# Down projections of a four-part feed-forward as seven block products, with weight sums made by adding DMAs

## The chip, the cores and the metric

The kernel runs on one core of one Trainium2 chip. The metric is the device time of one execution in microseconds (us). Engines: TensorE (PE; PEld is its weight load), VectorE (DVE), ScalarE (ACT), GpSimd (POOL), SyncE (SP, which only issues DMAs here).

## What is computed

One inference step of a two-layer encoder over T = 640 tokens (512 of a new stream, 8 x 16 of running streams), D = 1024, all in float32. The reference holds four feed-forwards (two in each layer), differential attention in the first layer, forgetting attention in the second, a shared K/V projection between them, and a final norm. What matters here:

```
def swiglu(x, w_gate, w_up, w_down):
    return (jax.nn.silu(x @ w_gate) * (x @ w_up)) @ w_down
...
x = x + 0.5 * swiglu(rms_norm(x, g), w_gate, w_up, w_down)    # w_gate, w_up: 1024 x 2816, w_down: 2816 x 1024
```

## The kernel before

**Numbers and halves.** Every matmul works on rounded parts: a weight and an operand are each split into a high part (a ScalarE copy to fp32r) and a low part (a VectorE subtraction), and hi x hi, hi x lo and lo x hi are added in PSUM. A product of 128 x 128 weights with half of the tokens (320) is thus three matmuls, of 320 columns each. The norm's root (rB) is multiplied in after the matmul, as it is one factor per token.

**A feed-forward** (f = 0 to 3) goes through 11 pairs of 128-wide hidden blocks in four groups of 2, 3, 3 and 3 pairs (GROUPS). For each group come first the gate and up columns, then the down projection of that group, which is added to the residual xT.

**Gate and up: sets of seven products.** A set is 256 columns of gate (even s) or up (odd s). Its weights are seen as a 2 x 2 of blocks W11, W12, W21, W22 (rows 0 to 511 and 512 to 1023 by 128 columns each), the tokens as two halves, and seven products in place of eight give the result. Their weights are the ROLES: W11, W12, W22 and the sums S1 to S4; their operands are called "1" to "7" (sums of parts of x, made once for each feed-forward). VectorE makes the four sums in `role_sum` (L2018), ScalarE the high parts in `role_high` (L1446), VectorE the low parts in `role_low` (L2004). Each role has one slot (ROLE_SLOT), which is free again when its product of the set before is through. `products` (L78) writes the order out: product S4 and product W22 of set s stand between those of set s + 1. TensorE's product is L780. Between products ScalarE copies a partial sum from one PSUM bank to another (`copy_rows`, L1526), which the next product then adds to: three copies for each set, and S2, S3 and W22 wait for them. VectorE reads the results in `first_rows`, `sums_out` and `last_rows`; ScalarE makes the silu (L1542) and the hidden high part (L1549), VectorE the hidden low part (L2196).

**Down: plain.** For each of eight output tiles of 128 rows, `ffn_down` (L886) multiplies all hidden blocks of the group with their weights, three matmuls for each block and token half. VectorE then scales with rB (L2246), adds half of it to xT (L2248) and, in the last group, goes on to the next operand (`low`, L1979, and the sum of squares, L1990), as ScalarE does in `finish` (L1420, L1425).

**Order.** Each engine's program is written out by hand; the class `Plan` counts what each semaphore has reached. All queues are in order: a waiting instruction holds back what is behind it. SP loads the weights into two raw buffers in turn (`load_ffn`, `set_load`); a raw buffer is free when its last split is done. GpSimd does nothing in the feed-forwards; it splits the weight tiles of qkv, kv and qb (L657, L659) and serves attention.

## Time and profile before

| | |
|---|---|
| median of 3 runs | 2509.86 us (2508.21 to 2512.95) |
| the profiled execution, its own time | 2508.48 us |
| its span | 2506.2 us |
| TensorE busy | 2457.8 us, 98% of the span, 18869 matmuls |
| VectorE, ScalarE, GpSimd busy | 1696.2, 1136.8 and 193.6 us |
| granted TensorE clock | 0.997 |
| HBM read, written | 246.56 MB, 13.51 MB |

The busy times overlap between engines. The chain of waits goes back from the last instruction to whatever released each step; an engine's idle time costs only where it stands on that chain.

### The profile page before, as it was taken

The page shows a single profiled execution, that of the slowest core. Times are in us where ns is not written, and L with a number is a line of the kernel's source. Part 1 is how long each engine was busy: PE and PEld are TensorE (multiplying, and loading weights), DVE is VectorE, ACT ScalarE, POOL GpSimd, SP SyncE. Part 2 cuts the span into 40 slices and gives each one's busy share as a digit, 9 for nine tenths or more (in the row PEclk, how much of TensorE's full clock was granted, in tenths as well). Part 3 has the DMA queues.
Part 4 walks back from the last instruction along what each step waited for, and adds up shares of the span by engine and source line. Part 5 has one row for each costly group of instructions (what it writes and reads, how often), then busy time and mean ns, then how long its engine had stood idle before and what let it go on. Part 6 is the DMA issues. An engine that isn't in the chain of part 4 may idle for free.

```text
span 2506.2 us, 46841 instructions
## 1 busy us (share of the span) xinstructions
PE 2457.8 (98%) x18869; PEld 2332.4 (93%) x18869; DVE 1696.2 (68%) x2966; ACT 1136.8 (45%) x2263; POOL 193.6 (8%) x140
## 2 busy tenths in 40 slices
PE   8999999999998999999999999999999999999998
PEld 8999999888678999999988999999996699999998
DVE  7777677322787876767624886858628787868585
ACT  6443444201785644434422643435418754535254
POOL 0000000344000000000054000000131000000000
PEclk9999999999999999999999999999999999999999
DMA  4323232232863132323224232322257531322222
GB/s 129 92 72 95 70 100 60 76 118 93 293 235 96 60 101 64 98 65 97 66 73 139 95 110 60 104 80 77 72 179 254 215 109 47 112 79 74 87 72 80
DMA packets 261489, 262.99 MB, mean 105 GB/s; under 512 B 13537, under 2 KB 222106, under 8 KB 261282
## 3 DMA queue, kind: packets, MB, share of 16 engines
q1 hardware_dynamic: 255536, 244.98, 31.4%
q10 hardware_dynamic: 5746, 15.12, 1.7%
q8 instruction: 146, 2.39, 0.4%
q14 instruction: 61, 0.50, 0.1%
HBM read 246.56 MB, written 13.51 MB: 104 GB/s over the span
## 4 chain that ended last, share of the span: by engine, by line
PE 90%; DVE 5%; ACT 3%; issue 2%; DMA 0%; POOL 0%; ACTq 0%; DVEq 0%; POOLq 0%
PE PS L780 40%; PE PS L886 24%; PE PS L967 10%; PE PS L730 7%; PE PS L718 2%; PE PS L1168 1%; PE PS L713 1%; PE PS L1025 1%; PE PS L1126 1%; PE PS L1087 1%; ACT R L1681 0%; ACT tt L1689 0%; DVE x_area L2063 0%; DVE tt L2375 0%; DVE R L2018 0%
## 5 line engine op out<-in xcount | busy, mean ns | idle before, releaser
L780 PE MATMUL PS<-x_area,w_area 128*128 128x320 f32 x3096 | 482.1, 309 | 0.0
L780 PEld LDWEIGHTS PS<-x_area,w_area 128*128 128x128 f32 x3096 | 461.0, 188 | 0.2 <-DVE w_area L2004 0.2
L886 PE MATMUL PS<-r_area,w_area 128*128 128x320 f32 x2568 | 393.3, 309 | 0.0
L886 PEld LDWEIGHTS PS<-r_area,w_area 128*128 128x128 f32 x2568 | 380.6, 188 | 0.8 <-DVE r_area L2196 0.8
L1446 ACT ACTIVATE w_area<-R 128x512 fp32r<-128x512 f32 x341 | 212.9, 629 | 200.6 <-PE PS L780 133.4
L1995 DVE TENSOR_TENSOR w_area<-R,w_area 128x768 fp32r<-128x768 f32 (+2 forms) x145 | 134.8, 929 | 218.9 <-ACT w_area L1431 217.4
L2004 DVE TENSOR_TENSOR w_area<-R,w_area 128x512 fp32r<-128x512 f32 x341 | 233.9, 686 | 47.6 <-ACT w_area L1446 41.5
L1431 ACT ACTIVATE w_area<-R 128x768 fp32r<-128x768 f32 (+2 forms) x145 | 119.1, 822 | 310.1 <-PE PS L886 283.1
L967 PE MATMUL PS<-w_area,xn_hi 128*128 128x512 f32 x800 | 252.1, 396 | 2.7 <-POOL w_area L659 2.7
L886 PE MATMUL PS<-v_area,w_area 128*128 128x320 f32 x1620 | 253.5, 309 | 0.0
L886 PEld LDWEIGHTS PS<-v_area,w_area 128*128 128x128 f32 x1620 | 241.5, 188 | 0.3 <-DVE v_area L2196 0.3
L2018 DVE TENSOR_TENSOR R<-R 128x512 f32<-128x512 f32 x336 | 230.3, 685 | 4.0 <-DMA R<-in_w_ffn_gate_dram 1.6
L780 PE MATMUL PS<-k_area,r_area 128*128 128x320 f32 x1296 | 206.8, 309 | 0.0
L2004 DVE TENSOR_TENSOR r_area<-R,r_area 128x512 fp32r<-128x512 f32 x259 | 177.2, 689 | 40.4 <-ACT r_area L1446 37.7
L1446 ACT ACTIVATE r_area<-R 128x512 fp32r<-128x512 f32 x259 | 161.7, 625 | 86.9 <-DVE R L2018 78.3
L780 PEld LDWEIGHTS PS<-k_area,r_area 128*128 128x128 f32 x1296 | 194.3, 188 | 0.3
L967 PEld LDWEIGHTS PS<-w_area,xn_hi 128*128 128x128 f32 x800 | 147.7, 189 | 31.5 <-POOL w_area L659 2.8
L657 POOL CAST w_area<-R 128x1024 fp32r<-128x1024 f32 x48 | 53.4, 1113 | 1560.6 <-PE PS L886 950.6
L1526 ACT ACTIVATE PS<-PS 128x320 f32<-128x320 f32 x258 | 106.8, 418 | 135.4 <-PE PS L780 134.9
L780 PE MATMUL PS<-x_area,r_area 128*128 128x320 f32 x1032 | 165.4, 309 | 0.5 <-issue 0.5
L967 PE MATMUL PS<-w_area,xn_lo 128*128 128x512 f32 x400 | 156.7, 392 | 0.0
L780 PEld LDWEIGHTS PS<-x_area,r_area 128*128 128x128 f32 x1032 | 154.8, 188 | 0.7 <-issue 0.7
(302 smaller groups left out, 3569.9 us busy)
## 6 DMA issues: line engine op xcount, KB each, us to landing
R<-in_w_ffn_up_dram SPq DMA_DIRECT2D x88, 512.0 KB, 3.9
R<-in_w_ffn_gate_dram SPq DMA_DIRECT2D x84, 512.0 KB, 3.9
R<-in_w_ffn_down_dram SPq DMA_DIRECT2D x96, 384.0 KB, 3.2
vreg<-in_cache_a_v_dram SPq DMA_DIRECT2D x8, 2048.0 KB, 9.0
vreg<-in_cache_b_v_dram SPq DMA_DIRECT2D x8, 2048.0 KB, 8.8
R<-in_cache_a_k_dram SPq DMA_DIRECT2D x14, 1024.0 KB, 6.8
R<-in_cache_b_k_dram SPq DMA_DIRECT2D x14, 1024.0 KB, 8.8
R<-in_w_qkv_a_dram SPq DMA_DIRECT2D x24, 512.0 KB, 3.8
```

The lines of the kernel that those rows point to most:

```text
L657: pool.tensor_copy(w_hi[slot][:, 0:words], raw[slot][:, 0:words]).then_inc(w_hi_made, 1)
L718: return pe.transpose(dst, src[rows], cst[rows, IDENT + 64 * r:IDENT + 64 * r + 64])
L730: last = pe.matmul(out[:, h, :], a[slot][:, w], x[:, k, h * HT:(h + 1) * HT], start=(k == 0 and a is w_hi and x is x_hi), stop=(k == kb - ...
L780: last = pe.matmul(PS[:, bank, 0:HT], a[:, k, :], b[:, k, :], start=(start and k == 0 and a is hi and b is x_hi), stop=(k == 3 and a is lo ...
L886: last = pe.matmul(out[:, h, :], a[slot][:, w], x[:, h * HT:(h + 1) * HT], start=(k == 0 and a is w_hi and x is hi), stop=(k == n - 1 and ...
L967: last = pe.matmul(PS[:, t, :], x[:, k, cols], a[s][:, w], start=(k == 0 and x is xn_hi and a is w_hi), stop=(k == KB - 1 and x is xn_lo))
L1431: act.activation(w_hi[p][:, 0:words], raw[p][:, 0:words], ACT.Copy).then_inc(w_cast, 1)
L1446: act.activation(role_parts(f, g, s, role)[0], role_source(f, g, s, role), ACT.Copy).then_inc(sem("early_cast") if key in EARLY_COUNT else ...
L1526: act.activation(PS[:, to, 0:HT], PS[:, of, 0:HT], ACT.Copy).then_inc(sem("copied"), 1)
L1995: dve.tensor_tensor(w_lo[p][:, 0:words], raw[p][:, 0:words], w_hi[p][:, 0:words].bitcast(F32), ALU.subtract).then_inc(w_split, 1)
L2004: dve.tensor_tensor(lo, role_source(f, g, s, role), hi.bitcast(F32), ALU.subtract).then_inc(sem("early_split") if key in EARLY_COUNT else ...
L2018: dve.tensor_tensor(*at, ALU.add).then_inc(w_summed, 1)
```

## The change

1. *Down projections* of all groups but the last one of the last feed-forward (PLAIN) become sets of the same kind. A down set is 256 output rows; there are four (DOWN_SETS) for each group, with a contraction over the group's pairs, so 2 or 3 blocks deep (`depth`) in place of 4. The operands "1" to "7" are now made from the hidden rows for each pair (`hidden_sum`, `hidden_parts_low`, `hidden_cast`): four sums, five casts (parts 1, 5, 7 with 6, 2 with 3, 4) and five low parts. The 0.5 and rB are multiplied into the gate (`gate_scaled`), and VectorE adds the results straight to xT.
2. *One chain of sets* runs through a whole feed-forward (`chain`). The down set that opens a group's down part does not interleave with the set before it: TensorE first finishes the last up set (S4, W22), then takes W11, S1, S2, W12, S3 of the down set (`opening_down`).
3. *Weight sums.* S1 = W21 + W22, S3 = W11 + W21 and, for gate and up, S4 = S2 + W12 are made by DMAs that GpSimd issues and that add a block from DRAM to one that lies in SBUF (`add_sums`). VectorE keeps S2 = S1 + W11, S4 of the down sets, and S1 of the first set in three feed-forwards. S2 and S4 share one buffer (`sums`), so the S2 sum of a set waits for the S4 split of the one before.
4. *Ends.* In the last group of feed-forwards 0 to 2, the next operand's tiles are made two at a time at the end of a down set (`finish_tile`, `finish_one`), and the following projection starts with `set_done` waits. The first two tiles of kv and qb are split by ScalarE and VectorE.
5. *Room.* kT (2560 KB) is stored to DRAM after kv and loaded back in qb; mask and rope constants are loaded by ScalarE's queue when qkv begins.

```diff
+DOWN_SETS = KB // 2
+PLAIN = ((3, len(GROUPS) - 1),)
+HIDDEN_PARTS = ("1", "5", "7", "2", "4")
...
-        self.tiles("kv", ROW_TILES)
+        self.tiles("kv", ROW_TILES, range(2))
...
+            def add_sums(f):
+
+                def first_sum(at):
...
+                    pool.wait_ge(w_loaded[p], PLAN.landed[key])
...
+                    pool.dma_start(role_source(*key, "S1"), weight_block(*key, 1, 1), accum_op=ALU.add).then_inc(sem("first_added"), 16)
+
+                def third_sum(at):
+                    key = (f, *at)
+                    pool.wait_ge(w_summed, PLAN.sum[(*key, "S2")])
+                    if (*key, "W11") not in EARLY_COUNT:
+                        pool.wait_ge(w_split, SPLIT[(*key, "W11")])
...
+                    pool.dma_start(role_source(*key, "S3"), weight_block(*key, 0, 1), accum_op=ALU.add).then_inc(sem("third_added"), 16)
...
+                order = chain(f)
+                first_sum(order[0])
+                for at, then in zip(order, order[1:] + [None]):
+                    third_sum(at)
+                    if then is not None:
+                        first_sum(then)
+                    fourth_sum(at)
...
+            def opening_down(f, g, s):
+
+                i = PLAN.set[f, g, s]
+                q, v, first_rows = s % 2, 2 + s % 2, 4 + s % 2
+                pe.wait_ge(sem("sum_read"), i - 1)
+                product(f, g, s, "W11", "1", q, True)
+                product(f, g, s, "S1", "5", v, True)
+                pe.wait_ge(sem("copied"), 3 * i + 1)
+                product(f, g, s, "S2", "6", q, False)
+                product(f, g, s, "W12", "2", first_rows, False)
+                pe.wait_ge(sem("copied"), 3 * i + 2)
+                product(f, g, s, "S3", "7", q, False)
...
             sp.wait_ge(w_used, BASE["qb"])
-            sp.wait_ge(stored, STORED["bv"])
+            sp.wait_ge(stored, STORED["kt"])
...
+            sp.dma_start(kT[:, :, :].rearrange("p h t -> p (h t)"), k_scr).then_inc(sem("v_back"), 16)
```

**ScalarE after an up part of three pairs (feed-forward 0, group 1).** From the cast of W11 of the second down set (D1) on; L1630 is the cast of a role, L1727 of a hidden part, L1715 a PSUM copy; `third_added` is the adding DMA of S3. Of the change:

```order
L1630 ACTIVATE r_area<-R2 128x384 [waits w_used,w_loaded1]
L1630 ACTIVATE w_area<-R1 128x384 [waits w_used,w_summed]
L1727 ACTIVATE v_area<-vN 128x320 [waits hidden_ready]
L1630 ACTIVATE r_area<-R2 128x384 [waits w_used,first_added]
L1715 ACTIVATE PS<-PS 128x320 [waits sum_read,w_used]
L1630 ACTIVATE r_area<-R1 128x384 [waits w_used,w_summed]
L1630 ACTIVATE w_area<-R2 128x384 [waits w_used,w2_loaded0]
L1630 ACTIVATE w_area<-R2 128x384 [waits w_used,w2_loaded1]
L1630 ACTIVATE w_area<-R2 128x384 [waits w_used,third_added]
L1715 ACTIVATE PS<-PS 128x320 [waits last_rows_read,w_used]
L1715 ACTIVATE PS<-PS 128x320 [waits first_rows_read,w_used]
```

The last two rows, D0's third and D1's first PSUM copy, stand behind the cast that waits for the adding DMA. Before, ScalarE had at this place the casts of plain down tiles (L1431) and two hidden high parts (L1549):

```order
L1526 ACTIVATE PS<-PS 128x320 [waits sum_read,w_used]
L1534 ACTIVATE R1<-PS 128x320 [waits sum_read,w_used]
L1446 ACTIVATE w_area<-R2 128x512 [waits w_used,w2_loaded1]
L1542 ACTIVATE tt<-tt 128x640 [waits gate_ready]
L1526 ACTIVATE PS<-PS 128x320 [waits last_rows_read,w_used]
L1431 ACTIVATE w_area<-R2 128x768 [waits w_used,w_loaded0]
L1549 ACTIVATE v_area<-tt 128x640 [waits hidden_ready] x2
```

**VectorE at the same place.** L2491 and L2499 are hidden sums, L2520 hidden low parts, L2268 role low parts, L2286 weight sums, L2479 the last up rows. Of the change:

```order
L2491 TENSOR_TENSOR vN<-tt 128x320 [waits dve_step,first_rows_read]
L2499 SCALAR_TENSOR_TENSOR vN<-tt 128x320
L2499 SCALAR_TENSOR_TENSOR vN<-tt,vN 128x320 [waits dve_step]
L2520 SCALAR_TENSOR_TENSOR v_area<-vN,v_area 128x320 [waits hidden_hi]
L2479 TENSOR_TENSOR tt<-tt,PS 128x320 [waits last_rows_read,w_used]
L2499 SCALAR_TENSOR_TENSOR vN<-tt,vN 128x320 [waits hidden_ready,last_rows_read]
L2520 SCALAR_TENSOR_TENSOR v_area<-vN,v_area 128x640 [waits hidden_ready,hidden_hi]
L2520 SCALAR_TENSOR_TENSOR r_area<-tt,r_area 128x640 [waits hidden_hi,dve_step,last_rows_read]
L2268 TENSOR_TENSOR r_area<-R2,r_area 128x384 [waits w_cast]
L2268 TENSOR_TENSOR w_area<-R1,w_area 128x384 [waits w_cast]
L2520 SCALAR_TENSOR_TENSOR v_area<-vN,v_area 128x320 [waits hidden_hi]
L2286 TENSOR_TENSOR R1<-R2 128x384 [waits first_added,w_split]
```

The last row is the S2 sum of D1, which releases the adding DMA for S3; it stands behind the sums and low parts of the last pair. Before, the same place had:

```order
L2169 TENSOR_TENSOR tt<-PS,R1 128x320 [waits fifth_copied,copied,w_used]
L2170 TENSOR_TENSOR tt<-PS,R1 128x320
L2178 TENSOR_TENSOR tt<-tt 128x640 [waits silu_done,sum_read,last_sum_read]
L2188 TENSOR_TENSOR tt<-tt,PS 128x320 [waits last_rows_read,w_used]
L2196 SCALAR_TENSOR_TENSOR v_area<-tt,v_area 128x640 [waits hidden_hi] x2
```

Two hidden low parts (x2) were all that followed the up rows there.

## Rows read from the trace of the kernel before

**Rows 1.** The page, section 1: busy time, share of the span, instructions

```profile
PE 2457.8 (98%) x18869; PEld 2332.4 (93%) x18869; DVE 1696.2 (68%) x2966; ACT 1136.8 (45%) x2263; POOL 193.6 (8%) x140
```

**Rows 2.** The chain of waits: start us, us, what; feed-forward 0, then qkv

```profile
102.89 73.92 PE PS L780 x504
176.81 42.24 PE PS L886 x288
...
451.37 13.64 PE PS L967 x60
```

**Rows 3.** Windows view, an up stretch and a down stretch of three pairs

```profile
core 0: us, PE busy (x) PEld busy (x) DVE busy (x) ACT busy (x) POOL busy (x), PEclk, DMA share, GB/s
102.89:176.81 73.92, 73.92 (x507) 73.92 (x506) 59.94 (x99) 39.21 (x73) 0.00 (x0) 1.00 0.24 69
176.81:219.05 42.24, 42.24 (x291) 42.24 (x290) 24.88 (x33) 10.13 (x14) 0.00 (x0) 1.00 0.35 106
```

**Rows 4.** Groups of VectorE, then ScalarE, by shape: busy us, mean ns | idle before

```profile
L2018 DVE TENSOR_TENSOR R<-R 128x512 f32<-128x512 f32 x336 | 230.3, 685 | 4.0 <-DMA R<-in_w_ffn_gate_dram 1.6
...
L2175 DVE TENSOR_TENSOR tt<-tt,rB 128x640 f32<-128x640 f32 x43 | 35.5, 826 | 4.8 <-DVE tt L2170 0.5
...
L1995 DVE TENSOR_TENSOR w_area<-R,w_area 128x1024 fp32r<-128x1024 f32 x17 | 20.8, 1223 | 4.4 <-ACT w_area L1431 4.4
...
L1446 ACT ACTIVATE w_area<-R 128x512 fp32r<-128x512 f32 x341 | 212.9, 629 | 200.6 <-PE PS L780 133.4 <-DVE R L2018 67.1
...
L1526 ACT ACTIVATE PS<-PS 128x320 f32<-128x320 f32 x258 | 106.8, 418 | 135.4 <-PE PS L780 134.9 <-issue 0.5
...
L1425 ACT ACTIVATE tt<-xT 128x640 f32<-128x640 f32 x47 | 34.0, 723 | 0.0
...
L1420 ACT ACTIVATE xn_hi<-xT,gT 128x640 fp32r<-128x640 f32 x24 | 20.0, 831 | 62.2 <-DVE xT L2248 62.2
```

**Rows 5.** Timeline of VectorE: start us, us, engine, line, operation

```profile
229.62 0.48 DVE L2156 TENSOR_TENSOR tt<-PS,rB 128x320 f32<-128x320 f32 x1
230.02 0.68 DVE L2018 TENSOR_TENSOR R<-R 128x512 f32<-128x512 f32 x1
230.62 1.47 DVE L2004 TENSOR_TENSOR w_area<-R,w_area 128x512 fp32r<-128x512 f32 x2
...
234.20 0.82 DVE L2175 TENSOR_TENSOR tt<-tt,rB 128x640 f32<-128x640 f32 x1
234.94 0.68 DVE L2004 TENSOR_TENSOR w_area<-R,w_area 128x512 fp32r<-128x512 f32 x1
```

**Rows 6.** DMA view: issues, KB each, median us to landing

```profile
R<-in_w_ffn_gate_dram SPq DMA_DIRECT2D x84, 512.0 KB, 3.9
R<-in_w_ffn_down_dram SPq DMA_DIRECT2D x96, 384.0 KB, 3.2
...
R<-in_w_ffn_down_dram SPq DMA_DIRECT2D x32, 256.0 KB, 2.8
...
vN<-out_dram SPq DMA_DIRECT2D x1, 2048.0 KB, 9.0
...
R<-in_x_sample_dram SPq DMA_DIRECT2D x4, 128.0 KB, 7.1
...
R<-in_w_f_b_dram SPq DMA_DIRECT2D x1, 64.0 KB, 2.2
```

**Rows 7.** Timelines of TensorE and VectorE at the start

```profile
58.37 1.87 PE L780 MATMUL PS<-v_area,r_area 128*128 128x320 f32 x11 [1.69 <-DVE r_area L2004]
...
57.63 0.68 DVE L2004 TENSOR_TENSOR r_area<-R,r_area 128x512 fp32r<-128x512 f32 x1
```

**Rows 8.** Timelines of GpSimd in qkv, SP's queue and TensorE before attention B

```profile
466.29 2.33 POOL L659 TENSOR_TENSOR w_area<-R,w_area 128x1024 fp32r<-128x1024 f32 x1 [6.88 <-issue]
...
1847.00 0.38 SPq L635 DMA_DIRECT2D vN<-out_dram  x1
...
1869.69 0.49 PE L1025 MATMUL PS<-kT,R 64*128 64x128 f32 x4
```

More of the change, by code:

```diff
@@ L103, in __init__ @@
         self.ffn(2)
-        self.tiles("qb", SQ_TILES)
+        self.tiles("qb", SQ_TILES, range(2))
         self.tiles("ob", SQ_TILES, range(SQ_TILES))
@@ new lines, in ffn @@
+        order, turned, base = chain(f), self.loads % 2, self.units
+        if f == 0:
+            for s in range(2):
+                for role, slot in STANDARD[s]:
+                    self.role((0, 0, s, role), slot)
+                    self.own((0, 0, s, role))
+                    self.split[0, 0, s, role] = self.unit[0, 0, s, role] + 1
+            base = self.units
+        for (g, s), role in products(f):
+            slot = ROLE_SLOT[role]
+            self.role((f, g, s, role), slot[:2] + str(1 - int(slot[2])) if turned and len(slot) == 3 else slot)
@@ new lines, in ffn @@
+        for n, ((g, s), role) in enumerate(splits(f)):
+            self.split[f, g, s, role] = base + n + 1
+            self.own((f, g, s, role))
+        for g, s in ([(0, 0), (0, 1)] if f == 0 else []) + order:
+            key, early = (f, g, s), f in EARLY and (g, s) == (0, 0)
+            p = self.next_load(key, not early)
+            if not early:
+                self.halves[p] += 1
+                self.landed2[key] = 16 * self.halves[p]
+                for part, last in ((1, "S3" if (g, s) in order else "W21"), (2, "W22")):
+                    self.raw_free[key, part] = self.raws.get((p, part), 0)
+                    self.raws[p, part] = self.split[f, g, s, last]
@@ L169 @@
+        for g, pairs in enumerate(GROUPS):
+            for k in range(pairs):
+                self.pair[f, g, k] = len(self.pair)
+                parts = HIDDEN_PARTS if (f, g) not in PLAIN else range(2)
+                self.hidden.update({(f, g, k, x): len(self.hidden) + n + 1 for n, x in enumerate(parts)})
+            if (f, g) in PLAIN:
+                self.tiles((f, g), KB, range(KB))
 PLAN = Plan()
-UNIT, LOAD = PLAN.unit, PLAN.load
+UNIT, LOAD, SPLIT = PLAN.unit, PLAN.load, PLAN.split
@@ L826, in first_pair, with set_rest @@
                 pe.wait_ge(sem("first_gate"), 2)
[L828 to L832 removed]
+            def set_rest(f, g, s):
+                product(f, g, s, "S4", "3", 6, False)
+                pe.wait_ge(sem("copied"), 3 * PLAN.set[f, g, s] + 3)
+                product(f, g, s, "W22", "4", 7, False)
```

942 lines of the change are left out of this document (608 added, 334 removed).

## The prediction

> **What bounds the kernel now.** I read the page first: TensorE is busy 98% of the span [rows 1]. Busy matmuls could still hide pauses, so the second view is the chain of waits [rows 2]: in the feed-forward parts it is TensorE alone, 504 matmuls in 73.92 us and 288 in 42.24 us, both 0.1467 us each, without a pause between groups. The third is the windows view [rows 3]: in such a stretch VectorE is busy 59.9 of 73.9 us, ScalarE 39.2, GpSimd not at all, and the granted clock is 1.00, its 2.4 GHz level. So only fewer matmuls, or a stall of TensorE, move the time there. One pause exists at the start, 1.7 us [rows 7].
>
> **What goes.** A pair of hidden blocks (256 wide) needs 8 output tiles x 2 blocks x 3 partial products x 2 halves = 96 down matmuls now; as four sets of seven products with three partial products each it needs 84. 41 of the 44 pairs change: 41 x 12 = 492 matmuls, at 0.1467 us [rows 2] **72.2 us less** on the path. Also 255 of the 344 weight sums (0.685 us; 336 are of one form, [rows 4]) leave VectorE, and 240 operations that update x; both lie beside TensorE now and save nothing by themselves.
>
> **What comes beside TensorE.** The spacing of independent VectorE operations is 0.40 us for 320 columns, 0.60 for 512 and 0.74 for 640 [rows 5]; by these ends 0.47 for 384 and 0.34 for 256 (my interpolation). A down set of three pairs takes TensorE 63 x 0.1467 = 9.24 us and VectorE 7 low parts and 2 sums of 384, 6 additions of 320: 6.6 us. With two pairs it is 6.16 against 5.5 us. That fits, so I cost the work itself at nothing; what costs is the order in which it has to come.
>
> **The price of an adding DMA, X**, from the sum on VectorE that releases it to its landing, is in no row. Plain loads land in 2.8 us for 256 KB, 3.2 for 384 and 3.9 for 512, in rows of 1 KB; 64 KB take 2.2 [rows 6]. The changed DMAs carry 128, 192 (down) and 256 KB (up). Lowest bound: a plain load of the same bytes, 2.4 / 2.6 / 2.8 us. But they also read their destination: a load of twice the bytes gives 2.8 / 3.2 / 3.9. They move pieces of 512 bytes, half of today's: if the part above 2.1 us, about what 64 KB take, doubles once more, 3.5 / 4.3 / 5.7. The far bound is the 7.1 us in which 128 KB land in the crowded first microseconds [rows 6]. I take a point a third of the way from the second to the third triple, **3.0 / 3.6 / 4.5**, since some of that slope is waiting behind other loads. The Trainium skill, DMA: Bandwidth & Descriptors (Anatomy of one DMA), gives a GpSimd DMA about 2.0 us plus its bytes at 436 GB/s; by that, as an estimate, X is 2.3 / 2.45 / 2.6 and the time that of the cheap rival below. No run here shows it.
>
> **Where TensorE will wait.** Count from the end of product S3 of the last up set of a group (0).
> - *Opening.* The S3 weights of the first down set D0 can only be split now (0.47 + 0.5 us); then VectorE does the gate scaling 0.74, sum S4 0.47, a low part 0.40, the up rows 0.8 and a dependent 0.83 (spacing and durations of [rows 4, 5]), hidden sums 5, 7, 6 (1.4 with their dependence) and low part 5: 6.2 us. TensorE has meanwhile S4 and W22 (3.52 us), W11 of D0, and S1 but for the last pair: 5.7 us with three pairs, 4.8 with two. It waits 0.6 or 1.4 us. Low part 7 is ready at 8.0, TensorE at 7.6 or 7.2: 0.4 or 0.9. Together **1.0 us** (three pairs) or **2.3 us** (two).
> - *Second down set D1.* After low 7 VectorE does low 2, W11, S4, low 4 and then the S2 sum of D1, ready at 10.6 (10.2). Only now may the adding DMA for its S3 start. ScalarE's cast of S3 waits for it, and behind that cast in ScalarE's queue stand the two PSUM copies, of which the second releases S2 of D1: 10.6 + X + 1.35 us. TensorE is there at 8.5 + 5 products = 15.1 (12.9 with two pairs: 10.2 + X + 1.25). It waits for X - 3.15, or X - 1.45: 0.45 or 1.55 us.
> - *The loop.* From the landing of one S3 sum to the next S2 sum VectorE and ScalarE take about 3.5 us in order; with X that is 7.1 against a set of 9.24 us, nothing; with two pairs 6.45 against 6.16, 0.3 us, twice. The next up set's 256 KB sum starts from the same loop and has room for 3.2 us: X = 4.5 costs 1.3. Later up sets have 12.3 us per set against X + 5 to 6.3, nothing.
> - So a three-pair opening costs 1.0 + 0.45 = 1.45 us, eleven of them **16.0**; a two-pair one 2.3 + 1.55 + 0.6 + 1.3 = 5.75, four of them **23.0**.
> - *Last group of the first three feed-forwards.* After each S3 cast ScalarE now makes two tiles of the next operand: 2 x (0.83 + 0.72) us [rows 4], one square waiting for VectorE, so the PSUM copies come 3.0 us later and the next sum later too. Room is left for X up to 2.65 at D2 and 2.15 at D3: 0.95 + 1.45; then the first weight tile of the next projection is split late (1.06 + 1.22 us against two products of 1.32, behind that work): 1.0. 3 x 3.4 = **10.2**.
> - *Start.* VectorE's split of a weight releases TensorE there [rows 7]. It loses two sums of 0.6 and gains two scalings of 0.74 and, ahead of the next split, four hidden sums and five low parts instead of two, less one S4 sum: 0.3 + 0.4 + 2.7 - 0.6, with dependences **3.3 us** more pause.
> - *Keys through DRAM.* 2560 KB more come back behind the values in SP's queue, issued at 1847.0 us; 2048 KB of values take 9.0 us to land, so with the 512 KB of the running streams all three land at about 1847.0 + 22.5 = 1869.5, and the first scores start at 1869.7 [rows 6, 8]: **1.0**, bounds 0 and 6. The store itself has two up sets, 24.6 us, before the first wait for it: nothing.
> - Masks and rope constants loaded later, and GpSimd relieved of two tiles each in kv and qb: covered by the first projection tiles, which take TensorE 13.6 us in qkv [rows 2], nothing; without that cover up to the 6.9 us that GpSimd's first subtraction is late in qkv [rows 8].
>
> **Sum.** -72.2 + 16.0 + 23.0 + 10.2 + 3.3 + 1.0 = -18.7. The profiled execution took 2508.5 us (span 2506.2), the median of the runs is 1.4 above: 2509.9 - 18.7 = **2491 us**.
>
> **Rivals.**
> 1. *Adding DMAs are cheap.* X = 2.8 / 3.2 / 3.9 makes the costs 11.6 + 18.2 + 7.8 + 4.3 = 41.9 and the time 2480; X of the plain loads makes them 11 + 13 + 4.4 + 4.3 = 32.7 and the time 2470. For it: the queues are busy only a quarter to a third of the time [rows 3]. Against it: a destination has to be read as well.
> 2. *Slower: the adding DMA decides.* The sum crosses zero near X = 3.5 / 4.2 / 5.6, since about 30 places (D1 of each group, the loop of the two-pair groups, D2 and D3 of the last) each take every further microsecond. At 3.5 / 4.3 / 5.7: 23.7 + 33.8 + 14.4 + 4.3 = 76.2, 2514. One microsecond above: 34.7 + 49.8 + 20.4 + 4.3 = 109.2, 2547. For it: software makes these descriptors, pieces are half as long, and they queue beside 1 MB of loads per set. The Trainium skill, Advanced Engine Details and Errata (DGE: Hardware vs Software), puts the first byte of the GpSimd path at about 1 us against 0.6; that would add some 0.4 to X and the forecast would lose most of its gain. Nothing here shows it.
> 3. *All is hidden:* my chains are too strict, and nearly the whole 72 us come, 2440. Against it: the queues are in order, and the sums above rest on rows.
> That the change does not do what it says is excluded: its program has 492 fewer matmuls of 320 columns.
>
> **Chances.** Forecast, 2480 to 2505: 0.33. Rival 1: 0.20, rival 3: 0.02. About no change: within 0.2% (5 us, what a measurement of this kernel can tell): 0.07. Rival 2 beyond it: 0.38. So faster 0.55, same 0.07, slower 0.38. The range leaves out half of rival 1's plain end with rival 3, and the far half of rival 2: **2465 to 2525**.
>
> **What would show it.** Right: the chain in an up stretch still 0.1467 us per matmul; pauses of TensorE at each first down set's S1 and S2 (about 1 or 2.3 us) and at the second set's S2, released by ScalarE's copy behind the S3 cast; the cast waits for the DMA. Adding DMAs from the down weights land in 3 to 4 us. Wrong: landings over 4.5 us (rival 2) or under 2.8 (rival 1); pauses inside up sets; a start pause far from 5 us; no pause at D1.

## The result, and the profile after

The changed kernel takes 2642.9 us (median of 4 runs, 2639.0 to 2651.5) against 2511.1 us before (median of 4 runs, one more than above), **5.3% slower** (ratio 1.053, 95% interval 1.050 to 1.056). The prediction was 2491 us, with a range of 2465 to 2525. The profiled execution has a span of 2639.8 us against 2506.2, so it shows 133.6 us to be explained.

The page of the changed kernel, parts 1, 3 (queues: packets, MB, share) and 6 (KB each, us to landing), against [rows 1] and [rows 6]:

```profile
PE 2445.3 (93%) x18377; PEld 2287.3 (87%) x18377; DVE 1831.0 (69%) x3624; ACT 1320.0 (50%) x2870; POOL 660.4 (25%) x507
...
q1 hardware_dynamic: 213072, 246.97, 29.6%
q0 software_dynamic: 178544, 88.37, 27.3%
...
R<-in_w_ffn_up_dram SPq DMA_DIRECT2D x88, 512.0 KB, 5.9
R<-in_w_ffn_down_dram SPq DMA_DIRECT2D x96, 384.0 KB, 4.8
R<-in_w_ffn_up_dram POOLq DMA_DIRECT2D x129, 256.0 KB, 6.8
R<-in_w_ffn_down_dram POOLq DMA_DIRECT2D x88, 192.0 KB, 5.0
R<-in_w_ffn_down_dram POOLq DMA_DIRECT2D x32, 128.0 KB, 4.1
```

The 492 matmuls are gone (18869 to 18377), but TensorE is busy 93% of the span, not 98%. Queue q0 is new: the adding DMAs. Plain loads beside them land later than in [rows 6]: 5.9 us for 512 KB against 3.9, 4.8 for 384 KB against 3.2.

The windows view of one up part and one down part of three pairs, against [rows 3]:

```profile
core 0: us, PE busy (x) PEld busy (x) DVE busy (x) ACT busy (x) POOL busy (x), PEclk, DMA share, GB/s
111.62:195.43 83.81, 78.52 (x518) 77.20 (x517) 62.38 (x112) 42.48 (x86) 25.02 (x20) 0.98 0.75 137
195.43:233.06 37.63, 35.12 (x236) 34.33 (x235) 31.77 (x67) 19.42 (x42) 11.10 (x9) 1.00 0.59 121
```

The up part holds 516 matmuls (504 of its own and 12 left over from the down set before), 75.7 us at 0.1467; it takes 83.8. The down part takes 37.6 us where the plain one took 42.2, and would take 34.3 (234 x 0.1467). So the surprise is in the up part, in which no matmul was saved. The DMA share rose from 0.24 to 0.75.

The waits view (us in total, times, longest):

```profile
DVE w_area L2268 <- ACT w_area L1630: 289.8, 192, 8.9
ACT w_area L1630 <- DMA R<-in_w_ffn_gate_dram: 213.4, 75, 5.6
ACT w_area L1630 <- DMA R<-in_w_ffn_up_dram: 207.3, 82, 8.9
...
PE PS L919 <- ACT PS L1715: 122.4, 90, 9.5
ACT w_area L1630 <- DMA R<-in_w_ffn_down_dram: 116.4, 53, 4.1
```

ScalarE's casts (L1630) wait for adding DMAs, VectorE's low parts (L2268) for the casts, and TensorE (L919) for PSUM copies that stand behind the casts in ScalarE's queue (L1715). More of it belongs to gate and up weights than to down weights.

**Where 133.6 us come from.** For each of the 10668 set matmuls (L919) I took the time from the start of the matmul before it to its own start, less 0.1467 us. The sum of these is 207.4 us: 169.9 where the trace shows a wait (97.8 in up sets, 72.1 in down sets; restarts of the pipeline are in it, so it is above the sum of the waits), 24.9 at the half clock without a wait, 12.6 spread. The four feed-forwards grew by 130.7 us (405.6 to 438.0, 427.9 to 458.6, 424.8 to 463.6, 422.5 to 451.3): 207.4, and 3.8 around the sets, less the 72.2 saved and the 8.4 that the kernel before had beyond its own 0.1467 per matmul. Everything else is +3. Below, this sum over the set matmuls is called the excess, and its part at waits the pauses.

**One turn of the loop.** Timelines of the four engines from U0 to U1, feed-forward 0, group 1 (U0 is the group's first up set). L799, L791 and L810 are the adding DMAs of S3, of S1 for the next set, and of S4; L2286 is the S2 sum:

```profile
122.15 0.69 DVE L2286 TENSOR_TENSOR R<-R 128x512 f32<-128x512 f32 x1
...
134.57 0.69 DVE L2268 TENSOR_TENSOR w_area<-R,w_area 128x512 fp32r<-128x512 f32 x1 [2.33 <-ACT w_area L1630]
135.30 0.69 DVE L2286 TENSOR_TENSOR R<-R 128x512 f32<-128x512 f32 x1
...
123.14 1.28 POOL L799 DMA_DIRECT2D R<-in_w_ffn_up_dram  x1 [8.06 <-DVE R L2286]
123.89 1.86 POOL L791 DMA_DIRECT2D R<-in_w_ffn_gate_dram  x1
124.64 2.43 POOL L810 DMA_DIRECT2D R<-in_w_ffn_up_dram  x1
...
127.96 0.63 ACT L1630 ACTIVATE w_area<-R 128x512 fp32r<-128x512 f32 x1 [3.41 <-DMA R<-in_w_ffn_up_dram]
...
133.91 0.63 ACT L1630 ACTIVATE w_area<-R 128x512 fp32r<-128x512 f32 x1 [4.12 <-DMA R<-in_w_ffn_up_dram]
...
135.60 0.41 ACT L1715 ACTIVATE PS<-PS 128x320 f32<-128x320 f32 x1
...
136.06 2.02 PE L919 MATMUL PS<-k_area,w_area 128*128 128x320 f32 x12 [1.20 <-ACT PS L1715]
```

After one S2 sum (122.15) all three DMAs go within 1.5 us: S3 waits for the sum itself, S1 stands behind S3 in GpSimd's queue, and S4 waits until S2 has been split. S3 has landed at 127.96, 4.8 us after its issue, S4 only at 133.91, 9.3 us after. The next S2 sum (135.30) writes the buffer in which S4 lies, and it also stands behind S4's low part (134.57) in VectorE's queue; no run here separates these two reasons. So a turn takes 2.5 us to the issue of S4, 9.3 to its landing and 1.4 through cast and split, 13.15 in all, where seven products take 12.3.

The source view gives min/median/max of the landings, of L799 (S3, all sizes) and then of L810 (S4, 256 KB):

```profile
DMA to landing us min/median/max: 3.2/4.5/11.0
```

```profile
DMA to landing us min/median/max: 4.4/8.3/10.9
```

By size the medians of S3 are 3.3, 3.8 and 4.6 us for 128, 192 and 256 KB, of S1 behind it 4.9, 6.3 and 7.2, of S4 8.3, all from the DMA's issue. The prediction had 3.0, 3.6 and 4.5, counted from the sum that releases the DMA. From the end of that sum to the issue it is 0.3 us more (122.84 to 123.14 above), so its X measures 3.6, 4.1 and 4.9.

### The profile page after: what moved, and what is told of

It is laid out like the page before. It is cut to its first block and busy times, and to the rows that moved or that the text cites. A ratio compares the mean times of both kernels' runs of the same rounds, so it can differ in the third digit from the quotient of the medians.

```text
span 2639.8 us, 48736 instructions
## 1 busy us (share of the span) xinstructions
PE 2445.3 (93%) x18377; PEld 2287.3 (87%) x18377; DVE 1831.0 (69%) x3624; ACT 1320.0 (50%) x2870; POOL 660.4 (25%) x507
## 3 DMA queue, kind: packets, MB, share of 16 engines
q0 software_dynamic: 178544, 88.37, 27.3%
## 5 line engine op out<-in xcount | busy, mean ns | idle before, releaser
L1630 ACT ACTIVATE w_area<-R 128x512 fp32r<-128x512 f32 (+2 forms) x583 | 328.3, 570 | 593.5 <-DMA R<-in_w_ffn_gate_dram 213.4
L2268 DVE TENSOR_TENSOR w_area<-R,w_area 128x512 fp32r<-128x512 f32 (+2 forms) x583 | 359.5, 617 | 290.8 <-ACT w_area L1630 289.8
L919 PE MATMUL PS<-x_area,w_area 128*128 128x320 f32 x3096 | 485.2, 310 | 4.4 <-ACT PS L1715 3.7
L919 PEld LDWEIGHTS PS<-x_area,w_area 128*128 128x128 f32 x3096 | 462.2, 188 | 6.8 <-ACT PS L1715 6.0
L2268 DVE TENSOR_TENSOR r_area<-R,r_area 128x512 fp32r<-128x512 f32 (+2 forms) x437 | 270.5, 620 | 87.8 <-ACT r_area L1630 76.5
L919 PE MATMUL PS<-r_area,w_area 128*128 128x320 f32 x1584 | 267.1, 314 | 30.6 <-ACT PS L1715 30.5
L1630 ACT ACTIVATE r_area<-R 128x512 fp32r<-128x512 f32 (+2 forms) x437 | 246.0, 564 | 82.7 <-DVE R L2286 32.2
L919 PEld LDWEIGHTS PS<-r_area,w_area 128*128 128x128 f32 x1584 | 243.7, 192 | 34.8 <-ACT PS L1715 34.8
L919 PE MATMUL PS<-r_area 128*128 128x320 f32 x1392 | 243.9, 315 | 32.0 <-ACT PS L1715 20.9
L919 PEld LDWEIGHTS PS<-r_area 128*128 128x128 f32 x1392 | 214.8, 191 | 41.1 <-ACT PS L1715 26.4
L919 PE MATMUL PS<-k_area,r_area 128*128 128x320 f32 x1440 | 240.1, 313 | 2.0 <-DVE k_area L2520 2.0
L919 PEld LDWEIGHTS PS<-k_area,r_area 128*128 128x128 f32 x1440 | 221.2, 191 | 2.8 <-DVE k_area L2520 2.5
L919 PE MATMUL PS<-v_area,w_area 128*128 128x320 f32 x960 | 180.8, 317 | 40.0 <-ACT PS L1715 40.0
L799 POOL DMA_DIRECT2D R<-in_w_ffn_down_dram x60 | 74.6, 1244 | 482.7 <-DVE R L2286 404.7
L919 PEld LDWEIGHTS PS<-v_area,w_area 128*128 128x128 f32 x960 | 151.7, 192 | 47.1 <-ACT PS L1715 47.1
L1715 ACT ACTIVATE PS<-PS 128x320 f32<-128x320 f32 x438 | 172.6, 410 | 21.8 <-PE PS L919 19.0
L919 PE MATMUL PS<-x_area,r_area 128*128 128x320 f32 x1032 | 165.9, 310 | 3.2 <-ACT PS L1715 1.9
L799 POOL DMA_DIRECT2D R<-in_w_ffn_up_dram x43 | 55.2, 1284 | 435.7 <-DVE R L2286 435.7
L919 PEld LDWEIGHTS PS<-x_area,r_area 128*128 128x128 f32 x1032 | 154.6, 188 | 4.8 <-ACT PS L1715 3.2
```

What stands on the lines that cost most here:

```text
L799: pool.dma_start(role_source(*key, "S3"), weight_block(*key, 0, 1), accum_op=ALU.add).then_inc(sem("third_added"), 16)
L919: last = pe.matmul(PS[:, bank, 0:HT], a[:, k, :], b, start=(start and opens), stop=(k == n - 1 and a is lo), skip_group_check=True)
L1630: act.activation(role_parts(f, g, s, role)[0], role_source(f, g, s, role), ACT.Copy).then_inc(sem("early_cast") if key in EARLY_COUNT else ...
L1715: act.activation(PS[:, to, 0:HT], PS[:, of, 0:HT], ACT.Copy).then_inc(sem("copied"), 1)
L2268: dve.tensor_tensor(lo, role_source(f, g, s, role), hi.bitcast(F32), ALU.subtract).then_inc(sem("early_split") if key in EARLY_COUNT else ...
```

## The experiments

Theory A: the burst of three adding DMAs behind one S2 sum, S4 last and sharing its buffer. Theory B, the prediction's: the landing of S3 ahead of two copies in ScalarE's queue. Theory C: the even load of the added bytes on the DMA engines. All times are medians. e1 to e4 ran on one chip one after another, so did e5 to e8, e9 to e11, and e13 to e15; the ratios are to the kernel before on the same chip.

| kernel | us | against before (95%) |
|---|---|---|
| e1_s4_vector | 2543.5 | 1.013 (1.011 to 1.014) |
| e2_copies_first | 2632.3 | 1.050 (1.048 to 1.052) |
| e3_gpsimd_sums | 2640.1 | 1.052 (1.050 to 1.053) |
| e4_vector_sums | 2532.9 | 1.009 (1.008 to 1.011) |
| e5_s1_before_s3 | 2836.0 | 1.130 (1.128 to 1.132) |
| e6_no_addition | 2497.4 | 0.995 (0.993 to 0.997) |
| e7_gpsimd_s4_first | 2567.8 | 1.023 (1.021 to 1.024) |
| e8_gpsimd_copy_first | 2561.9 | 1.021 (1.019 to 1.023) |
| e9_s3_alone | 2584.9 | 1.029 (1.028 to 1.031) |

### e1: S4 back to VectorE

```diff
-                    if is_down(*cur):
-                        role_sum(f, *cur, "S4")
+                    role_sum(f, *cur, "S4")
```

> One part undone: the S4 sums of the gate and up sets are made by VectorE again (as those of the down sets are), S1 and S3 stay adding DMAs. In the changed kernel TensorE stands still for 169.9 us in the sets (97.8 in up sets, 72.1 in down sets) and loses 24.9 us to the half clock. Theory A (burst): one S2 sum lets three adding DMAs go, S3, S1 of the next set, S4; they land one behind another, S4 last, about 9.3 us after its issue, and the next S2 sum has to wait for that since S2 and S4 share a buffer; that loop takes 13.1 us against a set of 12.3. With S4 on VectorE the loop is S3's and S1's alone, some 8 us, and the pauses in up sets fall from 97.8 to under 15, with most of the half clock: 2643 - 85 - 15 = about 2543. Theory B (queue position, the one of the prediction): the cast of S3 stands ahead of two PSUM copies, and S3's landing alone decides; then S4 matters only by a little load on the queues, and the time is 2615 to 2635. Theory C (the load on the DMA queues delays everything): a third of the added bytes goes, so about a third of the loss, 2590 to 2600.

Measured 2543.5. Pauses in up sets fell from 97.8 to 24.5 us (under 15 was expected), in down sets from 72.1 to 68.7, and the excess from 207.4 to 111.3. Waits and DMA views of e1:

```profile
PE PS L917 <- ACT PS L1713: 55.0, 49, 7.9
```

```profile
R<-in_w_ffn_up_dram SPq DMA_DIRECT2D x88, 512.0 KB, 5.0
R<-in_w_ffn_up_dram POOLq DMA_DIRECT2D x86, 256.0 KB, 5.5
```

86 of 375 adding DMAs, a quarter of the added bytes, carried 99 us, three quarters of the loss. That is A; B would have kept most of it and C two thirds. For the DMAs that stayed little changed: S3 lands as before (4.6 us at 256 KB), S1 after 6.7 us instead of 7.2. What e1 does not tell is whether S4 costs because it is the last of the burst or because of what waits for it: both went with it.

### e2: the copies ahead of the cast that waits

```diff
+                    if n and not finishing(prev):
+                        role_high(f, *cur, "S3")
...
-                        role_high(f, *then, "S3")
```

> Only ScalarE's order changes: the cast of S3, which waits for the adding DMA, stands behind the two PSUM copies (the third of the set before, the first of this set) instead of ahead of them; in the last group of the first three feed-forwards it stays where it was. All adding DMAs stay. Theory B (queue position): the 137 us in which TensorE waited for a copy go, and what remains is a wait for the S3 split itself, which TensorE needs only four products (7 us in up sets) later: 2540 or less. Theory A (burst): the loop from S2 sum to S2 sum is still 13.1 us against 12.3, so TensorE waits as long as before, now for a split: 2625 to 2645. In between where both hold: the down sets gain (72 us of pauses, most of them at D1 and later), the up sets do not: about 2600.

Measured 2632.3, 10.6 us less than the change. S4's landings in the source view, and TensorE's wait:

```profile
DMA to landing us min/median/max: 4.4/8.4/11.7
```

```profile
PE PS L919 <- ACT PS L1715: 104.9, 67, 8.2
```

S4 lands as late as before, and 86% of the wait for copies stays. The queue position is real and small: the pauses at D1's S2, 16.5 us in the change (D1 is the second down set of a group), are nearly gone, and 6.3 us came back at D1's S3.

### e6: the same DMAs without the addition

```diff
-..., weight_block(*key, 0, 1), accum_op=ALU.add).then_inc(sem("third_added"), 16)
+..., weight_block(*key, 0, 1)).then_inc(sem("third_added"), 16)
```

S1 and S4 are changed in the same way, so this kernel leaves out the sums and its products are not those of the reference; only its time is of use.

> The same DMAs from GpSimd, same blocks, bytes and places, without the addition: they overwrite the block in SBUF (the products S1, S3 and S4 are then made with W22, W21 and W12 in place of the sums). This asks what in the adding DMA is slow. Rival 1 (the addition, that is reading and adding at the destination): landings of 256 KB fall from 6.7 us to about 4, plain loads beside them from 5.8 to about 4.5, and the time to 2520 to 2550. Rival 2 (pieces of 512 bytes and descriptors made by software, which stay): landings stay above 6 us and the time at 2620 to 2645.

Measured 2497.4, ratio 0.995 (0.993 to 0.997): below both ends of the expectation, and the only kernel here that is faster than the one before. Page, parts 3 and 6, and the source view of S4:

```profile
q0 software_dynamic: 27568, 88.37, 12.5%
...
R<-in_w_ffn_up_dram POOLq DMA_DIRECT2D x129, 256.0 KB, 3.5
R<-in_w_ffn_down_dram POOLq DMA_DIRECT2D x88, 192.0 KB, 3.2
```

```profile
DMA to landing us min/median/max: 3.2/3.7/5.4
```

The same bytes from the same queue go in 27568 packets instead of 178544. Apart from 6000 of 4 bytes in each kernel, the packets of q0 in the two traces are all of 4096 bytes here and all of 512 bytes with the addition (median 159 ns against 65 ns each). They take 12.5% of the DMA engines' 2496 us against 27.3% of 2640, less than half, and S4 lands after 3.7 us instead of 8.3. All the rest is the same, so the addition costs 145.5 us. The 512-byte rows of the source are not by themselves what is slow: this kernel has them too. Whether adding DMAs with longer rows would go in larger packets was not tried. And even here, with the DMAs cheap and the order unchanged, only about 12 of the 72 us saved are left: its excess is 67 us.

### e5: S1 out of the burst

```diff
-                    third_sum(at)
                     if then is not None:
                         first_sum(then)
+                    third_sum(at)
```

> All adding DMAs stay, only GpSimd's order changes: the S1 sum of the next set is issued ahead of the S3 sum of this set, so that it need not start with the other two behind the S2 sum. Theory A (burst of three behind one S2 sum): the burst is two DMAs, the loop falls from 13.1 us by about a third of the 10.8 us that three take, to 9.5 to 10, under the 12.3 us of a set, and the pauses in up sets fall from 97.8 to about 25 as with S4 on VectorE: 2550 to 2570. Rival: the half on which the S1 sum waits has not landed yet at that place (plain loads take 5.9 us beside the adding ones), and the wait for it now holds S3 back: 2640 or more.

Measured 2836.0, ratio 1.130 (1.128 to 1.132): the rival, which had said 2640 or more, and 193 us above the change. GpSimd's waits, in whose queue S3 now stands behind:

```profile
POOL R L791 <- DMA R<-in_w_ffn_down_dram: 410.6, 52, 11.3
POOL R L791 <- DMA R<-in_w_ffn_up_dram: 376.7, 33, 84.1
```

A sum that is needed late and waits for a load must not stand ahead of one that is needed now.

### e3, e7, e8: GpSimd makes the sums itself

```diff
-                    pool.dma_start(role_source(*key, "S3"), weight_block(*key, 0, 1), accum_op=ALU.add)...
+                    pool.tensor_tensor(role_source(*key, "S3"), role_source(*key, "S2"), role_source(*key, "W22"), ALU.subtract)...
```

> No adding DMAs: GpSimd makes the same sums itself, S1 = W21 + W22 in place, S3 = S2 - W22, S4 = S2 + W12, at the same places of its program. A subtraction of 1024 columns took GpSimd 2.33 us, so 512 about 1.2 us, against 4.1 to 6.8 us of a landing. If the latency of the adding DMAs (A or B) is what costs: the pauses fall to those of the openings, 11 x 1.0 + 4 x 2.3 = 20 us, 2511 - 72 + 20 + 5 = about 2464, range 2455 to 2480. Theory D (the order around the down sets costs by itself, whoever makes the sums): openings and down sets keep most of their 72 us, 2500 to 2515. Rival E: GpSimd and VectorE slow each other down when both work in SBUF; VectorE then has operations longer than 0.69 us for 512 columns, and the time is anywhere up to 2600.

Measured 2640.1 with no adding DMA at all, the time of the change, and above everything that was expected. GpSimd's timeline (L793 is S1 of the next set, L814 S4):

```profile
241.49 1.29 POOL L793 TENSOR_TENSOR R<-R 128x512 f32<-128x512 f32 x1 [6.13 <-DMA R<-in_w_ffn_up_dram]
242.73 1.30 POOL L814 TENSOR_TENSOR R<-R 128x512 f32<-128x512 f32 x1
```

S4 takes 1.3 us, but stands behind an S1 that waits 6.1 us for a plain load. It is as late as the DMA made it, and TensorE loses as much (excess 215.5). e7 changes that order alone:

```diff
+                    fourth_sum(at)
                     if then is not None:
                         first_sum(then)
-                    fourth_sum(at)
```

> GpSimd makes the sums as in e3_gpsimd_sums, but in the order S3, S4, S1 of the next set. In e3 its S1 sum waited 5 to 6 us for the second half of the next set's load and the S4 sum stood behind it: S4 was made some 9 us after the S2 sum, as late as an adding DMA lands (242.7 against an S2 sum of about 233), and the pauses in up sets were 86 us. Theory A says that it is this lateness of S4, not the DMA as such, that costs: with S4 first the pauses in up sets fall to under 25, the half clock with them, and the time is 2640 - 65 - 40 = about 2535, 2520 to 2550. Rival (GpSimd and VectorE slow each other: 0.90 us for one form of low part against 0.69): VectorE is what is late, and the time stays above 2600.

Measured 2567.8, 72 us less; up pauses 86.0 to 37.5. With e1 this shows that in the up sets the time at which S4 is ready decides, whoever makes it. It stayed above the expected 2520 to 2550. Longer operations on VectorE go with that, but how much of the rest they explain was not isolated. VectorE's low parts in e7, the same form as 688 ns in the change:

```profile
L2272 DVE TENSOR_TENSOR w_area<-R,w_area 128x512 fp32r<-128x512 f32 x343 | 278.4, 824 | 2.4 <-ACT w_area L1634 2.2
```

e8 is e7 with the hidden casts behind the second PSUM copy:

```diff
+                        if not (is_down(*prev) or not prev[1] % 2 or (f, prev[0]) in PLAIN):
+                            rows_on(f, *prev, 0)
```

> As e7_gpsimd_s4_first, and in ScalarE's order the second PSUM copy and the copy of the fifth product stand ahead of the casts of hidden parts 5 and 7 (in e1_s4_vector the cast of part 5 waited 3.1 us for VectorE's hidden sum with the copy behind it, and TensorE's S3 waited 1.6 us for the copy). That place is U2 and U4 of each group, about 25 times. If it costs 1 us each: 20 to 25 us less than e7. Rival: VectorE's chain decides anyway (its fifth-copied sum waits), and the two are within 5 us.

Measured 2561.9, 6 us less instead of 20 to 25: the pauses at U2 and U4 fell by 21 us, but those at U5 and D0 grew by 11. That is close to the rival (within 5 us).

### e4 and e9: all sums on VectorE, and S3 alone by DMA

In e4 all four, in e9 all but S3 are VectorE's. The edit of e4:

```diff
-                        role_sum(f, *then, "S2")
+                        for role in SUMS[:2]:
+                            role_sum(f, *then, role)
                         role_low(f, *then, "S1")
+                        role_sum(f, *then, "S3")
```

> No adding DMAs: VectorE makes all four sums of each set (S3 as S2 - W22), block products in the down projections stay. VectorE gets 255 sums back, 0.69 us for 512 columns and less for 384 and 256. Up sets: VectorE had 59.9 of 73.9 us before the change in six sets, and now has the hidden sums too. If the adding DMAs cost it all and VectorE has room: pauses only at openings, about 2464 as with GpSimd's sums. Rival (VectorE becomes the bound of the down sets): 7 low parts, 4 sums and 6 additions are 7 x 0.34 + 4 x 0.34 + 6 x 0.4 = 6.1 us in a two-pair set of 6.16, and 7.6 in a three-pair set of 9.24, and openings have four more sums ahead of what TensorE waits for, 1.5 to 2 us each, 15 times: 2464 + 16 + 30 = about 2510.

Measured 2532.9: 110 us of the loss are gone with the DMAs, and 23 stay; the first expectation was 2464, the rival's 2510. Up pauses are 14.1 us, down pauses 67.7. An opening of a down part in e4, VectorE (L2282 sums, L2517 hidden low parts), ScalarE (L1707 copy) and TensorE:

```profile
997.46 0.48 DVE L2451 TENSOR_TENSOR tt<-PS,R 128x320 f32<-128x320 f32 x1
...
1000.69 0.48 DVE L2517 SCALAR_TENSOR_TENSOR v_area<-vN,v_area 128x320 fp32r<-128x320 f32 x1
...
1005.61 0.52 ACT L1622 ACTIVATE r_area<-R 128x384 fp32r<-128x384 f32 x1 [2.07 <-DVE R L2282]
1006.03 0.42 ACT L1707 ACTIVATE PS<-PS 128x320 f32<-128x320 f32 x1
...
1001.23 0.71 PE L911 MATMUL PS<-v_area,r_area 128*128 128x320 f32 x3 [1.69 <-DVE v_area L2517]
1003.09 0.71 PE L911 MATMUL PS<-v_area,r_area 128*128 128x320 f32 x3 [0.27 <-DVE v_area L2517]
...
1006.51 1.15 PE L911 MATMUL PS<-r_area,w_area 128*128 128x320 f32 x6 [1.40 <-ACT PS L1707]
```

VectorE's chain from the up rows (997.46) to the low part 5 (1000.69) is what the prediction's *Opening* described; the copy at 1006.03 waits behind a cast of D1 that waits for a sum.

> Only S3 is an adding DMA; S1 and S4 are VectorE's sums. In the changed kernel the S3 DMA, first of its burst, landed after a median of 3.34, 3.79 and 4.60 us (128, 192, 256 KB), close to the 3.0, 3.6, 4.5 of the prediction, and S1 and S4 behind it after 4.9 to 8.3 us. This kernel is the one that the prediction's sum described, one adding DMA in the loop. Theory A: landings of 3.3, 3.8, 4.6 and no up-set pauses; the prediction's terms with these prices are 18 + 27 + 11 + 4 = 60 us against 72 saved, 2498, and the two sums more on VectorE ahead of the openings add 0.5 to 1 us fifteen times: 2500 to 2515. Rival (the down sets' order costs more than the terms, as the 68 us of pauses there in e1_s4_vector and e4_vector_sums say): 2530 to 2540, as those two.

Measured 2584.9: both ends were wrong. S3 landed as forecast (3.3, 3.8 and 4.6 us), alone, and it costs 52 us against e4, in which VectorE makes it. The excess is 153.7 us against 103.7; 41 of the 50 are pauses, at many places of 0.3 to 2 us each (U4, U5, the two-pair and the last down sets). So the count of room was too generous even with one adding DMA in the loop, though e9 is not quite the kernel of the prediction: VectorE has S1 and S4 back. e1, with one adding DMA more and one sum less on VectorE, is 41 us faster. 32 of these are pauses, and the largest place is D0's S3, 18 us in e9 and none in e1: there TensorE waits for the second PSUM copy, which stands behind S1's cast, and that waits for a sum on VectorE, as in the lines of e4 above (17 us in e4). e9 also loses 13 us more at U4 and U5 and 11 less at D1's S2.

### e10 to e15: what the order at the openings costs

From here on S3 and S4 are on VectorE, except where stated.

| kernel | S1 | order | us | against before (95%) | mean clock, profiled |
|---|---|---|---|---|---|
| e10 | VectorE | copy 2 ahead of S1's cast, S4 sum late | 2530.9 | 1.009 (1.007 to 1.010) | 0.992 |
| e11 | DMA | as e10 | 2527.6 | 1.007 (1.006 to 1.008) | 0.993 |
| e12 | DMA | and the last pair's products last | 2514.6 | 1.001 (1.000 to 1.002) | 0.992 |
| e13 | DMA | and S3's near pairs ahead of W12's last | 2524.0 | 1.005 (1.004 to 1.007) | 0.984 |
| e14 | DMA, S3 too | as e13 | 2559.2 | 1.019 (1.018 to 1.021) | 0.985 |
| e15 | VectorE | as e13 | 2526.6 | 1.007 (1.005 to 1.008) | 0.986 |

The edit of e10 and e11 on ScalarE (and `role_sum(f, *cur, "S4")` of an opening set moved behind the hidden low part 2 on VectorE), then that of e12 on TensorE, then that of e13 to e15:

```diff
-                    if then is not None:
-                        role_high(f, *then, "S1")
                     if n >= 2:
                         copy_rows(f, *cur, 2)
...
+                    if then is not None:
+                        role_high(f, *then, "S1")
```

```diff
-                product(f, g, s, "S1", "5", v, True)
-                pe.wait_ge(sem("copied"), 3 * i + 1)
-                product(f, g, s, "S2", "6", q, False)
-                product(f, g, s, "W12", "2", first_rows, False)
+                for ks in (range(depth(g, s) - 1), (depth(g, s) - 1,)):
+                    product(f, g, s, "S1", "5", v, True, ks=ks)
+                    if 0 in ks:
+                        pe.wait_ge(sem("copied"), 3 * i + 1)
+                    product(f, g, s, "S2", "6", q, False, ks=ks)
+                    product(f, g, s, "W12", "2", first_rows, False, ks=ks)
```

```diff
+                product(f, g, s, "S3", "7", q, False, ks=near)
+                product(f, g, s, "W12", "2", first_rows, False, ks=last)
+                product(f, g, s, "S3", "7", q, False, ks=last)
```

> As e4_vector_sums (2533), with two changes of order. ScalarE makes the second PSUM copy (and the fifth) ahead of the cast of the next set's S1, which waits for a sum; VectorE makes the S4 sum of an opening down set after the hidden sums instead of ahead of them. In e4 TensorE waited for that copy at D0's S3 16.7 us in all, at D3's S3 and the up sets' S3 some 14, and at D0's S1 29 us, of which the S4 sum is 0.47 each time. If these waits go: 16.7 + about 8 + 7 = 32 us, 2501. Rival (VectorE is full there and the waits come back at the next product): within 10 us of 2533.

> As e10, but the S1 sums are adding DMAs, alone: an S1 sum waits for its own load alone and not for a sum on VectorE, so it can be early and its 3.8 to 4.6 us lie in no loop; VectorE loses 143 sums of 0.5 to 0.7 us. If the openings are bound by VectorE: 15 times 0.5 us and some of the two-pair sets, 8 to 12 us less than e10, 2490. Rival (S1 lands late, since its half is loaded late): slower than e10, 2510 or more.

e10 gave 2 us against e4 instead of 32: the wait at D0's S3 went (16.7 to 6.3 us), but U5's W22, 10.4 us, took its place, since its copy now came late. The rival was right. e11 gave 3 more instead of the 8 to 12 expected, and the intervals of the two overlap: an adding DMA costs nothing that can be seen where no loop goes through it.

> As e11 (2527.6), with the opening down set reordered on three engines. TensorE takes S1, S2 and W12 first for all pairs but the last, then for the last pair (6 matmuls of each before it needs the last hidden parts), then S3. ScalarE makes the third PSUM copy of the last up set ahead of two casts, the first copy of the opening set ahead of the cast of part 5, and the second ahead of the cast of S4. VectorE makes the low part of S3 after the hidden parts. In e11 TensorE lost at each opening of three pairs 0.91 (U5, W22) + 1.66 (D0, S1) + 0.43 (S2) + 0.58 (S3) us, 3.6 in all, eleven times, and 4 at those of two pairs. VectorE's chain of 6.3 us from the fifth rows to the low part 2 stays, so not all goes: about 0.85 + 1.6 = 2.4 us eleven times and 1.5 four times, 32 us: 2496, range 2488 to 2508; under 2504 it would beat both kernels. Rival (the waits come back at D1's W11 and S2, because VectorE's D1 sums are no earlier): 2515 to 2525.

13 us less than e11 instead of 32: TensorE no longer waits at S1, but now 1.3 us for the low part 2, the end of VectorE's chain. With 2514.6 us (ratio 1.0014) the block products come within 0.2% of the kernel before, and not below it.

> As e12 (2514.6; S1 by an adding DMA, S3 and S4 on VectorE), and in the opening down set TensorE takes S3 for all pairs but the last ahead of W12 for the last pair. In e12 TensorE waited 1.30 us at each opening for VectorE's low part 2 (which W12 of the last pair needs). S3's first pairs are 6 matmuls, 0.88 us: they cover that much of it where the second PSUM copy comes in time, 11 x 0.8 + 4 x 0.4 = 10 us: 2504. Range 2500 to 2510. Rival (the copy is late, as S2 of the last pair ends just before): no change, 2512 to 2517.

9 us slower than e12, outside the range and the rival, though its pauses are 63.1 us against 60.4. In the profiled executions, which differ by 14.5 us, the difference is the clock: 2 x (1 - 0.984) x 2526 = 81 us at the half level against 2 x (1 - 0.992) x 2511 = 40, and the excess at the half level is 23.4 us against 7.3. The clock fell at or just behind the pauses of D0 in 10 of the 15 openings of e13, and in 2 of 15 in e12, where W12's pause stands alone. TensorE at an opening in e13, one of the five at which the clock did not fall:

```profile
1004.42 0.70 PE L918 MATMUL PS<-v_area,r_area 128*128 128x320 f32 x3 [1.15 <-DVE v_area L2533]
1005.67 1.56 PE L918 MATMUL PS<-r_area,w_area 128*128 128x320 f32 x9 [0.55 <-ACT PS L1719]
```

> As e13, but S3 too is an adding DMA (S4 on VectorE); against e1_s4_vector (2543.5) only the order around the openings is new. If the order at the openings is what spends the gain: as much less as e13 is below e11 (about 24 us), 2520. If the landing of S3 (3.3 to 4.6 us in the loop) does: the freed time is waited for at D1 instead, 2530 to 2540. The difference to e13 is what S3 by DMA costs against S3 on VectorE.

> As e13, with S1 on VectorE as well (no adding DMA at all). e10 against e11 says that S1 on VectorE costs 3 us; at an opening VectorE's chain is what TensorE waits for, and S1 of D1 stands behind it. 2507 to 2515; if VectorE's room is the bound around D1 in the two-pair groups, up to 2520.

e14 and e15 came out above all that was expected of them (2559.2 and 2526.6). e14 against e13: S3 by DMA costs 35 us. D1's S2 alone waits 27.1 us in e14 and less than 1 in e13. What the opening gives back is waited for one set later, and more: e14 is 16 us above e1, which has the same sums in the old order. e15 against e13 points the same way as e10 against e11, 2 to 3 us for S1 by DMA, again with intervals that overlap. A second buffer, with the S2 sum ahead of S4's low part in VectorE's queue, so that S2 need not wait for S4, wasn't tried.

## Why the prediction was wrong

Its sum set 53.5 us of costs against 72.2 saved. The excess was 207.4.

| step | predicted | measured |
|---|---|---|
| fewer matmuls | -72.2 | -72.2 (18869 to 18377) |
| D0, three pairs, eleven times | 11.0 | 19.2 |
| D1, three pairs | 5.0 | 8.6 |
| D0, two pairs, four times | 9.2 | 9.7 |
| D1, two pairs | 6.2 | 8.6 |
| two-pair loop, D2 and D3 | 2.4 | 11.8 |
| last groups of feed-forwards 0 to 2 | 10.2 | 14.2 |
| start of feed-forward 0, with the old 1.7 | 5.0 | 6.3 |
| up sets of the three-pair groups | 5.2 | 75.2 |
| first up sets of feed-forwards 1 to 3 | 0 | 16.3 |
| half clock and scatter in the sets | 0 | 37.5 |
| keys through DRAM, qkv | 1.0 and 0 | 1.2 and 1.1 |

- **The step that failed** is in *The loop*: "Later up sets have 12.3 us per set against X + 5 to 6.3, nothing." It put one adding DMA in the loop. Three are in it: S3, the next S1 and S4 go within 1.5 us and land one behind another, and the next S2 sum waits for S4's split. Counted through S4, the turn is 2.5 + 9.3 + 1.4 us. The change's own text had all of it: three adding DMAs for an up set, two for a down set, one shared buffer. With S4 back on VectorE (e1), the pauses in the up sets of the three-pair groups are 4.6 us, as the prediction had for a loop without it (5.2).
- **X was 0.4 to 0.6 us too small** by the prediction's own count, from the end of the sum: 3.6, 4.1 and 4.9 us against 3.0, 3.6 and 4.5, for the first of a burst. Put into its terms this makes the costs 70.7 us and the time about 2508, no change, and still 134 us under the measured one. It was far more wrong as the price of each of three. Rival 2 had the right sign, and its signs came (landings over 4.5 us, 6.8 in the page for the up weights; pauses inside up sets), but it too priced one DMA at about 30 places: near its own turning point it leaves the same 134 us open. The down weights' adding DMAs landed in 4.1 and 5.0 us, where 3 to 4 was named as the sign of being right.
- The Trainium skill, DMA: Bandwidth & Descriptors (Anatomy of one DMA), gave 2.3, 2.45 and 2.6 us from issue to landing as an estimate. Without the addition e6 shows 2.6, 2.8 and 3.4 for S3, up to 0.8 above it; with the addition it is 3.3, 3.8 and 4.6.
- **The mechanism at D0 and D1 was right in place and cause** (VectorE's low parts, then the copy behind the cast of S3), and 11.8 us too small at three pairs and 2.9 at two. With X at 3.6 and 4.1, D1's rows would be 8.6 at two pairs, as measured, and 10.4 at three, against 8.6. D0 at three pairs pauses 15 us even in e6, where the DMAs are cheap, so there the chain on VectorE was mis-sized.
- **The two-pair loop** was 9.4 us too small. X at 3.6 gives 7.1 of the 11.8. S1 behind S3 is not the reason: with S3 alone by DMA (e9) the same place costs 13 us, with S1 alone (e11) nothing.
- **The first up sets of feed-forwards 1 to 3** (16.3 us) were put at nothing without a reason. About 11 us stay there in e6 and 7.5 in e4, so most of it is not the adding DMA; what it is was not taken apart.
- **Plain loads** were assumed to keep their landing times; 512 KB went from 3.9 to 5.9 us. That this is a separate part of the up sets' loss is not shown: e1 brought most of that loss back with loads still at 5.0.
- **The clock** was not in the sum. Beside the pauses, 24.9 us were lost at the half level; the mean granted clock was 0.982 against 0.997.

## What to carry to other kernels

Count everything that one event releases, not only the transfer that is looked for: what closes a loop can be the landing of the last of the burst, and a shared buffer or a place ahead in a queue makes the least urgent of them urgent. An adding DMA is cheap where it has a whole stage to land (S1 in e11) and dear inside a loop whose turn is as long as the bound engine's work. Where a structural change saves 3% of the matmuls but needs a join at each group, price the joins first: here D0 alone pauses 25 us with the DMAs cheap (e6) and 56 with all sums on VectorE (e4), and without any adding DMA, joins and sums together cost more than was saved.
